# Last stage of a two-layer MoE decoder: the residual joins in PSUM by identity products, square and norm read PSUM

## The reference, cut to what matters

```python
out = jnp.zeros((t, d), F32).at[tok_buf].add(y_buf.astype(F32) * w_buf[:, None])   # two weighted expert rows a token
h = h + out
y = h * lax.rsqrt(jnp.mean(h * h, axis=-1, keepdims=True) + EPS)
return y * final_norm
```

## Time and profile before

| | |
|---|---|
| median of 3 runs | 2073.36 us |
| the profiled execution, device time | 2069.8 us |
| its span in the profile | 2068.1 us |
| PE busy | 2005.8 us, 97% |
| DVE busy | 1576.0 us, 76% |
| ACT busy | 1338.0 us, 65% |
| mean granted TensorE clock | 0.995 |

### The profile page before, as it was taken

The page is one execution under the profiler, slowest core; times in us unless marked ns, Lnnn a source line. Parts: engine busy times, 40 slices in busy tenths (PEclk is TensorE's granted clock), DMA queues, the critical chain, the costliest instruction groups (busy, mean ns, idle before and its releaser), DMA issues. The chain is left out here.

```text
span 2068.1 us, 29817 instructions
## 1 busy us (share of the span) xinstructions
PE 2005.8 (97%) x10448; PEld 1636.6 (79%) x10448; DVE 1576.0 (76%) x1878; ACT 1338.0 (65%) x1818; POOL 277.5 (13%) x345
## 2 busy tenths in 40 slices
PE   7999998998999999999998989999899999999998
PEld 6888876887788888888886866777688888888885
DVE  4561235776888898889888357887898988889886
ACT  5332425663787878887873157664688777878784
POOL 2000000001211111111103422110211111112210
PEclk9999999999999999999999999999999999999999
DMA  4112222124999999999996020013799999999996
GB/s 142 41 58 86 71 75 88 72 75 179 350 384 390 388 389 386 382 376 383 387 358 214 1 78 25 22 62 113 267 390 385 383 385 387 387 387 386 383 356 258
DMA packets 123487, 513.24 MB, mean 248 GB/s; under 512 B 27373, under 2 KB 28490, under 8 KB 89610
## 3 DMA queue, kind: packets, MB, share of 16 engines
q1 hardware_dynamic: 103674, 474.11, 61.0%
q0 software_dynamic: 18576, 33.86, 4.3%
q10 hardware_dynamic: 1152, 4.19, 0.5%
HBM read 495.05 MB, written 50.86 MB: 264 GB/s over the span
## 5 line engine op out<-in xcount | busy, mean ns | idle before, releaser
L517 DVE TENSOR_TENSOR exp_w_lo<-ring_raw,first_w_hi 128x2048 fp32r<-128x2048 f32 x192 | 438.8, 2287 | 32.7 <-ACT first_w_hi L444 32.6
L517 DVE TENSOR_TENSOR exp_w_lo<-ring_raw,exp_w_hi 128x2048 fp32r<-128x2048 f32 x192 | 439.3, 2290 | 27.8 <-ACT exp_w_hi L444 27.7
L444 ACT ACTIVATE exp_w_hi<-ring_raw 128x2048 fp32r<-128x2048 f32 x192 | 367.8, 1918 | 60.4 <-PE exp_up_out L369 32.5
L444 ACT ACTIVATE first_w_hi<-ring_raw 128x2048 fp32r<-128x2048 f32 x188 | 360.5, 1918 | 60.9 <-PE exp_up_out L369 30.1
L314 POOL DMA_INDIRECT y_rows<-exp_y,base_rows_y x63 | 79.0, 1254 | 947.2 <-ACT exp_y L464 934.0
L369 PE MATMUL exp_gate_out<-exp_w_lo,exp_x_hi 128*128 128x512 f32 x512 | 199.8, 390 | 0.0
L369 PE MATMUL exp_y_out<-exp_w_lo,exp_hid_hi 128*128 128x512 f32 x512 | 199.6, 390 | 0.0
L369 PE MATMUL exp_up_out<-exp_w_lo,exp_x_hi 128*128 128x512 f32 x512 | 199.2, 389 | 0.0
L369 PE MATMUL exp_gate_out<-first_w_hi,exp_x_hi 128*128 128x512 f32 x272 | 109.3, 402 | 3.1 <-issue 2.0
L521 DVE TENSOR_TENSOR exp_x_lo<-exp_x_turned,exp_x_hi 128x1024 fp32r<-128x1024 f32 x62 | 75.9, 1224 | 47.6 <-ACT exp_x_hi L448 47.6
L369 PEld LDWEIGHTS exp_up_out<-exp_w_lo,exp_x_hi 128*128 128x128 f32 x512 | 96.1, 188 | 19.8
(11 more groups left out here) (535 smaller groups left out, 4632.2 us busy)
## 6 DMA issues: line engine op xcount, KB each, us to landing
ring_raw<-in_expert_w_gate_dram SPq DMA_DIRECT2D x128, 1024.0 KB, 10.9
ring_raw<-in_expert_w_up_dram SPq DMA_DIRECT2D x128, 1024.0 KB, 11.4
ring_raw<-in_expert_w_down_dram SPq DMA_DIRECT2D x128, 1024.0 KB, 11.3
l0w_raw<-in_ab_w_in_dram SPq DMA_DIRECT2D x48, 256.0 KB, 2.8
finish_y<-y_rows SPq DMA_DIRECT2D x8, 1024.0 KB, 12.7
ring_raw<-in_swa_w_qkv_dram SPq DMA_DIRECT2D x5, 1024.0 KB, 9.4
ring_raw<-y_rows SPq DMA_DIRECT2D x10, 512.0 KB, 4.4
base_h<-in_x_dram ACTq DMA_DIRECT2D x8, 512.0 KB, 6.8
```

The costliest lines, as they stand in the source:

```text
L444: nc.scalar.activation(split[split_slot(unit)][0][:], raw[raw_slot(unit)][:], ACT.Copy).then_inc(hi_ready, 1)
L517: nc.vector.tensor_tensor(lo[:], raw[raw_slot(unit)][:], hi[:].bitcast(F32), ALU.subtract).then_inc(lo_ready[split_slot(unit)], 1)
```

## The change

- VectorE's `rows(t)` runs in all eight tiles and signals `rows_added`; the k = 0 products and diagonals of the tiles 2, 4 and 6 go. The explicit drain behind `rows(t)` goes.
- After `multiply_last` a new step `residual(t)` waits for `rows_added` and adds `h[:, t]` (which by then holds the first-choice rows too) to `acc` by two float32 products with the identity, one for each half. These signal `summed`.
- `combine` goes from VectorE. ScalarE squares `acc` in place of `h`, and the norm reads `acc` in place of `h`. TensorE's wait before it uses a PSUM tile again is now for `made` (the norm) in place of `combined`.
- A pad keeps the later tiles at their addresses.

```diff
-    T, ACC, both = 8, 4, (2, 4, 6)
+    T, ACC = 8, 4
...
                 if t >= ACC:
-                    pe.wait_ge(combined, t - ACC + 1)
+                    pe.wait_ge(made, t - ACC + 1)
                 pe.wait_ge(y_ready[t], 16)
-                for k in (0, 1) if t in both else (1,):
-                    for b in range(2):
-                        cols = slice(b * BANK, (b + 1) * BANK)
-                        mm(acc[t % ACC][:, cols], diag[:, t, k], y[t][:, k, cols], start=(k == 0 or t not in both), stop=False)
+                for b in range(2):
+                    cols = slice(b * BANK, (b + 1) * BANK)
+                    mm(acc[t % ACC][:, cols], diag[:, t], y[t][:, 1, cols], start=True, stop=False)
...
-                before.multiply_last(t, [acc[t % ACC][:, 0:BANK], acc[t % ACC][:, BANK:]], False).then_inc(summed, 1)
+                before.multiply_last(t, [acc[t % ACC][:, 0:BANK], acc[t % ACC][:, BANK:]], False, stop=False)
+
+            def residual(t):
+                pe.wait_ge(rows_added, t + 1)
+                for b in range(2):
+                    cols = slice(b * BANK, (b + 1) * BANK)
+                    last = mm(acc[t % ACC][:, cols], c["ident"][:], h[:, t, cols], start=False, stop=True)
+                last.then_inc(summed, 1)
 
             for t in range(T):
                 rows(t)
                 last_rows(t)
+                residual(t)
...
             for t in range(T):
-                for k in (0, 1) if t in both else (1,):
-                    last = nc.scalar.activation(diag[:, t, k], c["ident"][:], ACT.Copy, scale=weight[:, k, t:t + 1])
+                last = nc.scalar.activation(diag[:, t], c["ident"][:], ACT.Copy, scale=weight[:, 1, t:t + 1])
...
             for t in range(T):
-                act.wait_ge(combined, t + 1)
-                nc.scalar.activation(junk[:], h[:, t], ACT.Square, accum_out=c["sums"][:, t:t + 1])
+                act.wait_ge(summed, t + 1)
+                nc.scalar.activation(junk[:], acc[t % ACC][:], ACT.Square, accum_out=c["sums"][:, t:t + 1])
...
             def rows(t):
-                if t not in both:
-                    dve.wait_ge(y_ready[t], 16)
-                    nc.vector.scalar_tensor_tensor(h[:, t], y[t][:, 0], weight[:, 0, t:t + 1], h[:, t], ALU.mult, ALU.add)
-                    dve.drain()
-
-            def combine(t):
-                dve.wait_ge(summed, t + 1)
-                nc.vector.tensor_tensor(h[:, t], h[:, t], acc[t % ACC][:], ALU.add).then_inc(combined, 1)
+                dve.wait_ge(y_ready[t], 16)
+                nc.vector.scalar_tensor_tensor(h[:, t], y[t][:, 0], weight[:, 0, t:t + 1], h[:, t], ALU.mult, ALU.add).then_inc(rows_added, 1)
...
-                nc.vector.scalar_tensor_tensor(h[:, t], h[:, t], scale[:, t:t + 1], gain[:], ALU.mult, ALU.mult).then_inc(made, 1)
+                nc.vector.scalar_tensor_tensor(h[:, t], acc[t % ACC][:], scale[:, t:t + 1], gain[:], ALU.mult, ALU.mult).then_inc(made, 1)
 
             rows(0)
             rows(1)
-            combine(0)
             for t in range(T):
                 if t + 2 < T:
                     rows(t + 2)
-                if t + 1 < T:
-                    combine(t + 1)
                 normed(t)
```

More of the change, by code:

```diff
@@ L611, in until_last_rows, with multiply_last @@
             engine.wait_ge(last_made, halves)
-        def multiply_last(t, outs, first, halves=(0, 1)):
+        def multiply_last(t, outs, first, halves=(0, 1), stop=True):
             for out, half in zip(outs, halves):
@@ L616, in multiply_last @@
                 for n, part in enumerate((last_hi, last_lo)):
-                    last = nc.tensor.matmul(out, hot[:, t], part[:, cols], start=(first and n == 0), stop=(n == 1))
+                    last = nc.tensor.matmul(out, hot[:, t], part[:, cols], start=(first and n == 0), stop=(stop and n == 1))
             return last
@@ L3198, in finish @@
         y = [mem.sb(f"y{j}", [P, 2, 1024]) for j in range(6)]
-        diag, gain, junk = mem.sb("diag", [P, T, 2, P]), mem.sb("gain", [P, 1024]), mem.sb("junk", [P, 1024])
+        diag, gain, junk = mem.sb("diag", [P, T, P]), mem.sb("gain", [P, 1024]), mem.sb("junk", [P, 1024])
         scale, root = mem.sb("scale", [P, T]), mem.sb("root", [P, T])
+        mem.sb("diag_pad", [P, T, P])
         mem.sb("pad", [P, 3 * 4096 - 2 * T])
@@ L3204, in finish @@
         y_ready = [mem.sem(f"y_ready{j}") for j in range(T)]
-        diag_made, summed, combined, rooted, gain_ready, made, stored = (
-            mem.sem(x) for x in ("diag_made", "summed", "combined", "rooted", "gain_ready", "made", "stored"))
+        diag_made, rows_added, summed, rooted, gain_ready, made, stored = (
+            mem.sem(x) for x in ("diag_made", "rows_added", "summed", "rooted", "gain_ready", "made", "stored"))
         def sync_early(sp):
```

## The result

The changed kernel took 2079.46 us (median of 9 runs, 2077.43 to 2081.24) against 2073.75 us for the kernel before (9 runs). The ratio is 1.0032, 95% interval 1.0022 to 1.0041. The forecast was 2080.0 us, a ratio of 1.0032.

What follows compares the result with a forecast made beforehand. The prediction took TensorE to bound the last stage, VectorE close behind. +8.6 (products) - 0.64 (waits filled) - 1.24 (combine) - 0.03 (square) = +6.7 us on 2073.36 gave 2080.0 us, 8 in 10 within 2077.0 to 2082.5.

Steps and rivals of the forecast that it cites:

- What bounds the stage: Last stage: TensorE (PE) bounds it, VectorE close behind; the loads hold up only the first tiles.
- Part 1: TensorE's products in the last stage: net 10 more float32 products of a half at 0.86 us, +8.6 us.
- Both bounds of the price: Price of one identity product of a half on TensorE: 0.86 us from above, 0.23 us (fp32r) from below.
- Part 2: PE's waits for loads in the last stage: longer tiles fill them, only tile 0's restart stays, -0.64 us.
- Part 3: Tail after PE's last product: tile 7's combine and its hand-over go, -1.24 us; the other seven bring nothing.
- Part 4: Tile 7's square and norm reading PSUM instead of SBUF: -0.03 us for the square, nothing for the norm.
- Part 5: New and moved waits in the last stage, such as PE's for rows_added and made: all have room, costing nothing.
- The rival of a pipeline emptied at each new wait: PE at residual(t) in each tile: 0.8 to 2.4 us on top, 2080.8 to 2082.4 us; chance 12%.
- The sum: Whole last stage: products, filled waits, combine and square together give +6.7 us, or +6.67 counted from the norm's end.
- a rival of 8% for a shift outside the stage: Outside the last stage: one build shifts against the other, median perhaps 2077 or below; 8%, 1% reaching faster.
- the signs named for being wrong: Profile after: tiles under 4.2 us, PE waits for rows_added or made, clock off 1.00, stage start not 2032.

Runs made afterwards that it cites:

- join_left_out: The changed kernel without its identity products, so residual and first-choice rows are missing from the result: stage 26.17 us, ratio to the kernel before 0.9981.
- rows_vector_all: The kernel before with VectorE adding the first-choice rows in all eight tiles, combine kept, no identity products: stage 33.89 us, ratio 1.0014.
- join_rounded: The changed kernel with VectorE's sum rounded to fp32r and fp32r identity products: stage 28.38 us, ratio to the kernel before 0.9986.
- both_all: The kernel before with both choices on TensorE in all eight tiles, combine kept, no identity products: stage 39.42 us, ratio 1.0039.
- join_last_only: The kernel before with the identity join in tile 7 alone and tile 6's first-choice rows moved to VectorE: stage 31.71 us, ratio 0.9998.
- the second comparison: The changed kernel run once more, unaltered, against the kernel before on one chip: stage 38.19 us, ratio 1.0023 (1.0012 to 1.0033).
- combine_into_psum: The kernel before with combine writing its sum into PSUM, and square and norm reading it there: stage 31.72 us, ratio 0.9997.

## Why the prediction was right, point by point

**What bounds the stage.** Right. PE is busy throughout before and after, and `join_left_out` and `rows_vector_all` show the two limits behind it, the loads (26.2 us) and VectorE (33.9 us with all rows on it).

**Part 1, the price of the products.** 1.72 us for two, as taken from L3242. The starts of neighbouring tiles are 4.35 or 4.36 us apart where 4.37 was forecast, and 4.44 behind tile 0, with its restart. Both bounds of the price were met in a run, for two products: 1.72 us in the change, 0.47 in `join_rounded`.

**Part 2, waits filled.** Right in kind: one wait of 0.3 us is left, for tile 0, ahead of the stage's first product. The size depends on the execution. Before's waits differed by 0.3 us between its two profiles, so the term is 0.6 to 1.0 us rather than 0.64. `y[2]` came 6.3 us behind the first product, a little later than I reckoned, which no longer mattered.

**Part 3, the tail.** 1.24 us forecast with 0.03 for the square; `both_all` less the change gives 1.23 to 1.28. Seven of eight combines taken away brought nothing, as VectorE's 12.5 us of waiting shows. One thing the working passed over: tile 7's `combine` at 2059.47 came as much behind VectorE's own norm (2058.18 and 1.28 us) as behind PE's sum, so the end of the kernel before had two limits at once. The sum holds because the change lifts VectorE's; `join_last_only`, which doesn't, gained nothing.

**Part 4, PSUM readers.** Groups of the changed kernel by line and shape (count, busy us, mean ns):

```profile
L3290 DVE SCALAR_TENSOR_TENSOR base_h<-finish_acc,finish_scale,finish_gain 128x1024 f32<-128x1024 f32 x8 | 10.3, 1284 | 0.6
...
L3275 ACT ACTIVATE finish_junk<-finish_acc 128x1024 f32<-128x1024 f32 x8 | 8.2, 1024 | 25.3 <-PE finish_acc L3253 25.3
```

The same two groups of the kernel before:

```profile
L3289 DVE SCALAR_TENSOR_TENSOR base_h<-base_h,finish_scale,finish_gain 128x1024 f32<-128x1024 f32 x8 | 10.3, 1284 | 0.6
...
L3268 ACT ACTIVATE finish_junk<-base_h 128x1024 f32<-128x1024 f32 x8 | 8.5, 1058 | 18.5 <-DVE base_h L3281 18.4
```

The norm takes 1284 ns from PSUM as from SBUF. The square fell from 1058 to 1024 ns, 0.034 us. From the cycles and clocks in the Trainium skill's table ("VectorE: DVE Perf Modes", "The TRN2 errata") I estimate 0.043 us between the two sources for ScalarE, near that. The 0.065 us the other way that the same table gives for VectorE doesn't show.

**Part 5, the new waits.** None shows on PE. The rival of a pipeline emptied at each new wait falls: from L617 to L3253 and from there to L3242 the starts follow without a gap.

**The sum.** +6.67 us for the stage, +6.55 by the first pair of profiles, +6.3 by the second. The runs gave +5.7 us by the medians and 6.6 by the ratio of the first comparison, 4.8 in the second. That the median came out 0.5 us from the forecast is in part luck: the runs of each kernel spread over some 4 us, and the second comparison differs from the first by 1.8 us. What the sum did not have is the scatter of the stage's start, up to 8 us, which is larger than the whole effect; there was only a rival of 8% for a shift outside the stage. One of the signs named for being wrong did come up, a start at another time than 2032: it was 2033.83 and 2035.50. It says nothing against the sum, since it came up in the kernel before as well (2033.21).

## What to carry to other kernels

Adding a tensor in PSUM by a product with the identity isn't free: in plain float32 it costs TensorE what any product of that shape does, here 0.86 us for 512 columns against 0.23 in `fp32r`, and in float32 it pays only where TensorE has that time to spare. Before work is moved between engines, add up each engine's work for a tile of the stage (here 2.65 or 4.37 us on TensorE, 2.7 or 4.0 on VectorE); where the two are balanced, moving it either way loses. What helped here was an idle third engine, or cheaper products where the precision may go. Reckon with a whole engine's sum, not with the last steps of the chain, also for a small swap in the tail.

## What the runs showed of the hardware that I had not expected

GpSimd's float32 add of 128 × 1024 takes 2.36 to 2.39 us where nothing holds it up, about twice VectorE's 1.22, and 3.36 us where it starts while VectorE's norm still runs on two SBUF tensors. A VectorE norm with two SBUF tensors is stretched beside it from 1.28 to between 1.87 and 2.18 us. With one tensor from PSUM instead, the norm (1.28 us) and `combine` (1.21 to 1.23) are not stretched at all. So a tile kept in PSUM, worth nothing in `combine_into_psum`, is worth 3.6 us of the stage once GpSimd works beside VectorE (32.58 against 28.96).

The clock fell to 1.2 GHz for short stretches in some executions and not in others, far ahead of the stage, in the stretch shown with the same instructions and waits on PE. The start of the stage, which scatters by 8 us, goes with the clock lost in this way (correlation 0.93 over 14 profiles).
